# Linear attention's queries, keys and decays with features on partitions, and the last stage of an encoder block begun ahead of the last expert's rows

## The chip, the cores and the metric

The kernel runs on one core of one Trainium2 chip, in float32. The metric is the device time of one execution in microseconds (us). Before the change the median of three runs is 1846.63 us (1843.77 to 1850.55).

## What is computed

One layer of a hybrid encoder over 2048 tokens of width 1024, and a last normalisation:

```python
u = rms_norm(x, norm1_w)
z = u @ w_in + b_in            # q_a k_a (256 each), v_a g_a (512 each), lr_a (16), q_b (512), k_b v_b (128 each)
log_a = log_sigmoid(lr_a @ gla_w_a2 + gla_b_a2) / 16
# gated linear attention, 4 heads, in chunks of 64 tokens:
b = cumsum(log_a, within the chunk)
q_dec = q_a * dk**-0.5 * exp(b);  k_inv = k_a * exp(-b);  k_end = k_a * exp(b_last - b)
att   = causal(q_dec @ k_inv.T)
o     = att @ v_a + q_dec @ state;  state = exp(b_last) * state + k_end.T @ v_a
# sliding-window attention of q_b, k_b, v_b with ALiBi and sinks, 8 heads, softmax
h = x + concat(norm_gate(o, g_a), o_b) @ w_out
h = h + hier_moe(rms_norm(h, norm2_w))      # top 1 of 4 groups, top 2 of its 8 experts (SwiGLU, 512 wide)
y = rms_norm(h, final_norm_w)
```

## The kernel before

Four stages follow each other.

**Mixer.** A software pipeline over 16 tiles of 128 tokens. In iteration i each engine runs its own program (`pe_iter`, `act_iter`, `dve_iter`, `pool_iter`, `sp_iter`); the part marked new or lag 0 works on tile i, the part marked old (lag 1) on tile i-1, and lag 2 on tile i-2. The table `JOBS` lists the PSUM results in the order in which TensorE makes them; result k goes into bank k % 8, and TensorE waits until the bank's former content has been read. In one iteration TensorE does, in this order: q and k of linear attention (`qk`, tokens on partitions, 8 matmuls 512 wide, `project`, L295), transposes of the decayed q and k (`qdki`, L338 and L340), transposes of h (`u2Ta`, `u2Tb`), the chunk's scores (`att0`, `att1`, L354), the state's increments (`dS0`, `dS1`, L365), then v, router, transposed softmax rows, g, the two attentions' outputs, k_b and v_b, q_b with the low-rank gate inside it (`la`, L458), the output projection (`wo0`, `wo1`, L323), the window's scores (`s0` to `s3`, L472), and last the cumulative sums of the log decays as matmuls with constant triangles (`bb`, L482) and their chunk ends (`bl`, L486).

VectorE (DVE) ends an iteration with the second half of `h_sb` (L796), the gate (L799), the window's scores into `sc` (L807), their maxima (L814 to L819, which gives `nm_ready`), and begins the next with `qd`, `ki` and `ke` (L684 to L686), q and k times the decays. ScalarE (ACT) computes the decays `E` after the gate's exponential (L585, L586), then the eight exponentials of the softmax (L593), which wait for `nm_ready`, and begins the next iteration with the copy of the transposed `qdkiT` out of PSUM (L508), for which `att0` waits.

**Routing** makes for each of the 32 experts a list of rows: 128 in full, and up to 32 more as quarters of rows.

**Experts.** A loop over 32 experts. SyncE (SP) streams the next expert's three matrices of 2 MB while TensorE multiplies: gate (L1190), up (L1201), down (L1226, and L1215 for more than 128 rows). GpSimd (POOL) gathers rows of the normalised `v2` and adds the results into `h_dram` by two indirect DMAs per expert (`put_back`, L1109).

**Last stage** (`finish`). It begins when all 32 experts' sums have landed:

```python
sp.wait_ge(sem("h_summed"), 1)     # POOL gives it once the last expert's sums have landed
fin_sp(sp)                         # loads h_dram in 4 pieces (L1333), stores 16 tiles (L1336)
```

ACT squares and sums each tile (L1348), adds epsilon (L1351), POOL takes the power -0.5 (L1341), DVE scales by it and the weight (L1357), and SP stores. The loaded tiles lie in the weights' buffer `wts` and in `h_rest`.

## Time and profile before

| | us |
|---|---|
| median of 3 runs | 1846.63 (1843.77 to 1850.55) |
| profiled execution | 1847.37 |
| its span in the profile | 1845.5 |
| TensorE busy | 1740.8 (94%) |
| DVE, ACT, POOL busy | 579.1, 522.4, 279.9 |
| mean granted TensorE clock | 0.976 of full speed |

In the page each engine's busy time is a share of the span; one engine near its whole span in a stretch bounds the stretch, and where none is, a wait or the DMA does. The mixer is in the first half of the span, the experts in most of the second, and the last stage behind TensorE's last matmul.

### The profile page before, as it was taken

Reading aid. Unit: us, or ns where it says so; the run is one execution under the profiler, and the core shown is the slowest. Engines: PE = TensorE matmul, PEld = TensorE weight load, DVE = VectorE, ACT = ScalarE, POOL = GpSimd, SP = SyncE. Lnnn points to the kernel's source line nnn. Section 1 sums busy time; section 2 is a strip of 40 time slices with the busy share of each in tenths; the row PEclk is TensorE's granted clock in tenths of the full one; section 3 lists DMA queues with packets and bytes.
Section 4 is the critical chain, followed back from the end, with each engine's and each line's share of the span. In section 5 each row is a group of like instructions: output and inputs, shape, how many; then the busy total and the mean of one; then the engine's idle time right before and its main releaser. Section 6 shows DMA issues by size and latency. Waiting matters only on the chain. (4 is left out here: it accounts for less than half of the span.)

```text
span 1845.5 us, 29515 instructions
## 1 busy us (share of the span) xinstructions
PE 1740.8 (94%) x10686; PEld 1233.6 (67%) x10687; DVE 579.1 (31%) x1521; ACT 522.4 (28%) x1317; POOL 279.9 (15%) x345
## 2 busy tenths in 40 slices
PE   7899999999999999999976999999999999999980
PEld 4556665566656666566645788878888888888860
DVE  1344344443455334553346111111111111111114
ACT  0444343443434433434334111111111111111114
POOL 0000011010110101001010122222221222222213
PEclk9999999999999999999987999999999999999995
DMA  9410011100111001111023889989999999999969
GB/s 351 108 58 35 29 51 57 57 34 23 57 57 57 34 23 57 57 48 43 23 87 131 271 275 339 298 291 319 335 317 300 304 336 316 312 311 311 304 198 366
DMA packets 130356, 321.92 MB, mean 174 GB/s; under 512 B 10723, under 2 KB 18804, under 8 KB 130324
## 3 DMA queue, kind: packets, MB, share of 16 engines
q1 hardware_dynamic: 113908, 278.78, 42.7%
q0 software_dynamic: 15552, 42.61, 9.2%
q8 instruction: 21, 0.34, 0.1%
q10 hardware_dynamic: 864, 0.10, 0.0%
q14 instruction: 11, 0.09, 0.0%
HBM read 274.27 MB, written 47.19 MB: 174 GB/s over the span
## 5 line engine op out<-in xcount | busy, mean ns | idle before, releaser
L295 PE MATMUL bank<-w_in_sb,uT 128*128 128x512 f32 (+1 forms) x1024 | 378.9, 524 | 2.3 <-DVE uT L659 2.3
L295 PEld LDWEIGHTS bank<-w_in_sb,uT 128*128 128x128 f32 x1024 | 176.0, 191 | 169.2 <-issue 169.2
L1190 PEld LDWEIGHTS bank<-xT,wts 128*128 128x128 f32 x2048 | 248.9, 191 | 25.2 <-issue 20.8
L1190 PE MATMUL bank<-xT,wts 128*128 128x128 f32 (+2 forms) x2048 | 253.3, 283 | 6.3 <-issue 5.2
L1201 PE MATMUL bank<-xT,wts 128*128 128x128 f32 (+2 forms) x2048 | 247.9, 282 | 0.0
L1201 PEld LDWEIGHTS bank<-xT,wts 128*128 128x128 f32 x2048 | 245.0, 191 | 0.0
L1226 PE MATMUL bank<-wts,hT 128*128 128x512 f32 x512 | 231.7, 595 | 0.0
L323 PE MATMUL bank<-w_out_sb,mixT 128*128 128x512 f32 x512 | 222.7, 592 | 1.5 <-ACT mixT L536 0.8
L1279 DVE TENSOR_TENSOR hT<-bank,sg 128x160 f32<-128x160 f32 x128 | 41.6, 325 | 444.2 <-PE bank L1201 444.2
L323 PEld LDWEIGHTS bank<-w_out_sb,mixT 128*128 128x128 f32 x512 | 96.0, 190 | 116.5 <-issue 114.3
L1226 PEld LDWEIGHTS bank<-wts,hT 128*128 128x128 f32 x512 | 92.2, 190 | 97.6 <-issue 97.6
L301 PEld LDWEIGHTS bank<-uT,w_in_sb 128*128 128x128 f32 x1280 | 147.9, 192 | 11.9 <-issue 11.6
L301 PE MATMUL bank<-uT,w_in_sb 128*128 128x128 f32 x1280 | 155.7, 277 | 0.0
L830 POOL TENSOR_SCALAR ss<-ss 128x1 f32<-128x1 f32 (+1 forms) x49 | 9.4, 191 | 826.0 <-ACT junk L579 428.6
L1245 ACT ACTIVATE y<-bank,gatec 128x256 f32<-128x256 f32 x32 | 15.2, 474 | 343.8 <-PE bank L1226 197.7
L1109 POOL DMA_INDIRECT h_dram<-y,putc x64 | 102.0, 1594 | 35.9 <-POOL putc L1116 26.2
L1116 POOL COPY putc<-put 128x2 int32 (+1 forms) x32 | 5.8, 182 | 535.2 <-DVE y L1287 535.2
L1236 ACT ACT_TABLE_LOAD x32 | 41.1, 1283 | 157.9 <-PE bank L1190 157.9
L1236 ACT ACTIVATE sg<-bank 128x160 f32<-128x160 f32 x128 | 38.9, 304 | 118.3 <-PE bank L1190 117.9
L593 ACT ACTIVATE sc<-sc,sm 128x192 f32<-128x192 f32 x128 | 56.3, 441 | 33.0 <-DVE sm L819 33.0
L579 ACT ACTIVATE junk<-h_sb 128x1024 bf16<-128x1024 f32 x16 | 16.9, 1057 | 138.1 <-DVE h_sb L796 138.1
L1287 DVE TENSOR_SCALAR y<-bank,gatec 128x512 f32<-128x512 f32 x32 | 24.0, 751 | 94.3 <-PE bank L1226 94.3
(231 smaller groups left out, 1745.8 us busy)
## 6 DMA issues: line engine op xcount, KB each, us to landing
wts<-w_gate_in SPq DMA_DIRECT2D x32, 2048.0 KB, 11.0
wts<-w_up_in SPq DMA_DIRECT2D x32, 2048.0 KB, 9.5
wts<-w_down_in SPq DMA_DIRECT2D x32, 2048.0 KB
x_sb<-x_in SPq DMA_DIRECT2D x17, 512.0 KB, 3.5
xT_in<-x_t_in SPq DMA_DIRECT2D x17, 512.0 KB, 4.4
w_in_sb<-w_in_in SPq DMA_DIRECT2D x4, 2048.0 KB, 11.8
h_sb<-x_in SPq DMA_DIRECT2D x16, 512.0 KB, 3.2
h_dram<-h_sb SPq DMA_DIRECT2D x16, 512.0 KB, 2.9
```

Source lines behind the costliest of these rows:

```text
L295: m = pe.matmul(bk[name][:, col:col + hi - lo], uT[:, k, :], w_in[:, k, lo:hi], start=k == 0, stop=k == KD - 1)
L301: m = pe.matmul(bk[name][0:hi - lo, col:col + P], w_in[:, k, lo:hi], uT[:, k, :], start=k == 0, stop=k == KD - 1)
L323: m = pe.matmul(bk[f"wo{n}"][:, :], mixT[:, k, :], w_out[:, k, n * 512:(n + 1) * 512], start=k == HA, stop=k == HA - 1)
L579: act.activation(junk[:, :], h[:, 1 - par, :], ACT.Square, accum_out=ss[:, 8:9]).then_inc(sem("ss2_ready"), 1)
L593: act.activation(sc[:, hh, :], sc[:, hh, :], ACT.Exp, bias=nm[:, hh:hh + 1], accum_out=sums[:, hh:hh + 1])
L1109: po.indirect_dma_start(out=table, out_offset=bass.IndirectOffsetOnAxis(ap=putc[:, col:col + 1], axis=0), in_=src, in_offset=None, compute ...
L1190: m = pe.matmul(G[m_ % 2][:, 0:w], wg[:, k, m_ * P:(m_ + 1) * P], xT[:, k, 0:w], start=k == 0, stop=k == KD - 1)
L1201: m = pe.matmul(U[m_ % 2][:, 0:w], wu[:, k, m_ * P:(m_ + 1) * P], xT[:, k, 0:w], start=k == 0, stop=k == KD - 1)
L1226: m = pe.matmul(YB[half][:, :], hT[:, k, 0:P], wd[:, k, half * 512:(half + 1) * 512], start=k == 0, stop=k == KF - 1)
L1236: act.activation(sg[:, m_, 0:n_], G[m_ % 2][:, 0:n_], ACT.Silu).then_inc(sem(pre + "sg_ready"), 1)
L1279: nc.vector.tensor_tensor(hT[:, m_, 0:n_], U[m_ % 2][:, 0:n_], sg[:, m_, 0:n_], ALU.mult)\
L1287: nc.vector.tensor_scalar(y[:, part, 512:D], (YB, G)[part][1][:, :], gatec[:, part:part + 1], None, ALU.mult)\
```

## The change

In the mixer, q and k of linear attention come out of TensorE with features on partitions and tokens along the row (four groups of 8 matmuls 128 wide, weights stationary), and the low-rank gate `la` likewise (2 matmuls 128 wide for 1 of 256). The cumulative sum within a chunk then runs along the row: a scan on DVE over 256 elements, with a constant `within` that is 0 at each chunk's start, in place of the matmuls `bb` and `bl`, and one more DVE operation for b_last - b. ACT's exponentials of the decays move from behind the gate's last exponential to ahead of the square of h. DVE multiplies q and k by the decays at the end of the same iteration, ahead of `sc`; the first two products are written straight into `qdkiT`, so that ACT's copy of it goes. Only the third, `keT`, is still transposed (2 transposes for 4), and ACT copies it to `ke` (256 wide for 512), for which `dS0` waits. One bias table of 9 columns replaces a broadcast of 256 KB, and two constants go.

At the end, the loops of ACT, DVE and POOL stop one expert earlier and the last expert is written out. SP loads h into a buffer of its own once the sums of the first 31 experts have landed (`m_y_put` at 32 * 31), and the 16 tiles are normalised and stored from it; rows of the last expert are stored in a stale form in this pass. The last expert's up to 160 rows of h are gathered by two indirect DMAs (`pool_base`), its results are added from PSUM in SBUF (`dve_base`), normalised there, and stored over the stale rows by two indirect DMAs (`pool_out`), which wait until all 16 tiles' stores have landed. Epsilon is added on POOL, and the power is taken for up to three tiles at a time. A branch `redo` repeats the stage where experts overflow.

```diff
 JOBS = [
-    ("qk", 0, {"qk_ready": (1, 1)}), ("qdki", 1, {"qdkiT_ready": (1, 1)}),
+    ("qk", 0, {"qk_ready": (1, 1)}), ("keT", 1, {"ke_ready": (1, 1)}),
...
-    ("bb", 0, {"decays_ready": (1, 1)}), ("bl", 0, {"dec_ready": (1, 1)}),
+    ("spare0", -1, {"uT_ready": (2, 2)}), ("spare1", -1, {"uT_ready": (2, 2)}),
...
-            project("qk", C_QK, C_V).then_inc(sem("qk_done"), 1)
...
+            for n in range(4):
+                m = project_T("qk", C_QK + n * P, C_QK + (n + 1) * P, n * P)
+            m.then_inc(sem("qk_done"), 1)
+        if on("keT"):
+            wait(pe, sem("keT_ready"), i)
+            transposes("keT", lambda c: keT[:, c * P:(c + 1) * P], 2)
...
-                    pe.matmul(bk["la"][:, 0:QKA], lrT[:, :], w_a2[:, :], start=True, stop=True).then_inc(sem("la_done"), 1)
+                    for n in range(2):
+                        la = pe.matmul(bk["la"][:, n * P:(n + 1) * P], w_a2[:, n * P:(n + 1) * P], lrT[:, :], start=True, stop=True)
...
-        if on("bb"):
...
-            for n in range(2):
-                m = pe.matmul(bk["bb"][:, n * QKA:(n + 1) * QKA], cums[:, n, :], ls[:, :], start=True, stop=True)
...
-                m = pe.matmul(bk["bl"][:, 2 * pr:2 * pr + 2], ls[:, pr * P:(pr + 1) * P], cind[:, :],
...
# act_iter
-            act.activation(qdkiT[:, :, :].rearrange("p a b -> p (a b)"), BK["qdki"][:, :], ACT.Copy)\
+            wait(act, sem("keT_done"), i)
+            wait(act, sem("dS_done"), 2 * (i - 1))
+            act.activation(ke[:, :], BK["keT"][:, 0:QKA], ACT.Copy).then_inc(sem("ke_ready"), 1)
...
+            wait(act, sem("cum_ready"), 2 * i + 2)
+            wait(act, sem("keT_ready"), i)
+            act.activation(E[:, 0, :], cum[:, :], ACT.Exp, scale=1.0 / 16.0)
+            act.activation(E[:, 2, :], cum[:, :], ACT.Exp, scale=-1.0 / 16.0)
+            act.activation(E[:, 1, :], E[:, 1, :], ACT.Exp, scale=1.0 / 16.0).then_inc(sem("decays_ready"), 1)
...
# dve_iter
+            dve.tensor_tensor_scan(cum[:, :], within[:, :], ls[:, :], 0.0, ALU.mult, ALU.add).then_inc(sem("cum_ready"), 1)
...
+            wait(v_, sem("decays_ready"), i + 1)
+            wait(v_, sem("og_done"), 2 * i)
+            wait(v_, sem("keT_done"), i)
...
+            dve.tensor_tensor(keT[:, :], qk[:, QKA:], E[:, 1, :], ALU.mult).then_inc(sem("keT_ready"), 1)
...
# finish
+    PIECES = ((0, 1), (1, 4), (4, 10), (10, 16))
+    ROOTS = ((0, 1), (1, 4), (4, 7), (7, 10), (10, 13), (13, 16))
...
+    def pool_base(po):
+        po.indirect_dma_start(out=base[:, :], in_=scratch["h"], out_offset=None, in_offset=at(main)).then_inc(sem("last_moved"), 16)
+        po.indirect_dma_start(out=base_t[:, :], in_=quarters(scratch["h"]), out_offset=None, in_offset=at(rest)).then_inc(sem("last_moved"), 16)
+
+    def dve_base(v_):
+        v_.wait_ge(sem("last_moved"), 32)
+        v_.wait_ge(sem("m_d_done"), 3 * NE - 1 + CREDIT)
...
+        v_.wait_ge(sem("m_d_done"), 3 * NE + CREDIT)
+        nc.vector.scalar_tensor_tensor(base[:, H:D], bank[7][:, :], weight[:, main], base[:, H:D], ALU.mult, ALU.add).then_inc(sem("last_summed"), 1)
...
+    def pool_out(po):
+
+        po.wait_ge(sem("out_stored"), 16 * NT)
+        po.wait_ge(sem("last_steps"), 5)
+        po.indirect_dma_start(out=A["out"], out_offset=at(main), in_=last[:, :], in_offset=None, bounds_check=SEQ - 1, oob_is_err=False)\
...
# SP, then ACT behind the loop over 31 experts
-            sp.wait_ge(sem("h_summed"), 1)
-            fin_sp(sp)
...
+            sp.wait_ge(sem("m_y_put"), 32 * (NE - 1))
+            fin_sp(sp, 0)
...
+            act_silu(act, "m_", NE - 1)
+            fin_act(act, 0, 0, 4)
+            act_squares(act, 0, 2)
+            fin_act(act, 0, 4, 6)
+            act_squares(act, 2, 3)
+            fin_act(act, 0, 6, NT)
```

On DVE, at the end of an iteration of the mixer's loop, the program of before reads (`sm` holds the maxima, `qd`, `ki`, `ke` the decayed products):

```order
L796 TENSOR_TENSOR h_sb<-bank,h_sb 128x512
L799 SCALAR_TENSOR_TENSOR g_t<-g_sb,g_t 128x512
L60 REGISTER_ALU
L807 SCALAR_TENSOR_TENSOR sc<-bank,alibi 128x2x192
...
L814 TENSOR_REDUCE sm<-sc 128x8
L816 TENSOR_TENSOR sm<-sm,sinks_sb 128x8
L818 TENSOR_TENSOR sm<-sinks_sb,sm 128x8
L819 TENSOR_SCALAR sm<-sm 128x8
L684 SCALAR_TENSOR_TENSOR qd<-qk_sb,decays 128x256
L685 TENSOR_TENSOR ki<-qk_sb,decays 128x256
L686 TENSOR_TENSOR ke<-qk_sb,decays 128x256
```

and that of the change, at the same place:

```order
L780 TENSOR_TENSOR h_sb<-bank,h_sb 128x512
L783 SCALAR_TENSOR_TENSOR g_t<-g_sb,g_t 128x512
L788 SCALAR_TENSOR_TENSOR qdkiT<-qk_sb,decays 128x256
L790 TENSOR_TENSOR qdkiT<-qk_sb,decays 128x256
L792 TENSOR_TENSOR keT<-qk_sb,decays 128x256
L60 REGISTER_ALU
L800 SCALAR_TENSOR_TENSOR sc<-bank,alibi 128x2x192
...
L807 TENSOR_REDUCE sm<-sc 128x8
L809 TENSOR_TENSOR sm<-sm,sinks_sb 128x8
L811 TENSOR_TENSOR sm<-sinks_sb,sm 128x8
L812 TENSOR_SCALAR sm<-sm 128x8
```

The three products moved from behind the maxima to ahead of the window's scores.

On ACT, from the gate's logarithm to the next iteration's first copy, before:

```order
L575 ACTIVATE g_t<-g_t 128x512
L579 ACTIVATE junk,ss<-h_sb 128x1024
L582 ACT_TABLE_LOAD
L582 ACTIVATE g_t<-g_t 128x512
L585 ACTIVATE decays<-bank 128x512
L586 ACTIVATE decays<-bank 128x256
L589 ACTIVATE dec<-bank 128x4
L593 ACTIVATE sc,sm<-sc,sm 128x192 x8
L594 ACTIVATE sm<-sm 128x8
L508 ACTIVATE qdkiT<-bank 128x512
```

and of the change:

```order
L558 ACTIVATE g_t<-g_t 128x512
L562 ACT_TABLE_LOAD
L562 ACTIVATE decays<-cum 128x256
L563 ACTIVATE decays<-cum 128x256
L564 ACTIVATE decays<-decays 128x256
L566 ACTIVATE dec<-cum 128x4
L570 ACTIVATE junk,ss<-h_sb 128x1024
L573 ACTIVATE g_t<-g_t 128x512
L576 ACTIVATE sc,sm<-sc,sm 128x192 x8
L577 ACTIVATE sm<-sm 128x8
L493 ACTIVATE ke<-bank 128x256
```

The decays and the table load moved ahead of the square of h (`junk,ss<-h_sb`), and the copy behind the softmax is now that of `ke`.

On ACT, what stands behind the loop over 31 experts in the changed program (`last_sum` and `last_quarters_sum` hold the last expert's rows); before, the silu rows `sg<-bank` were in the loop and the 16 squares stood behind it:

```order
L1231 ACTIVATE sg<-bank 128x160 x4
L1362 ACTIVATE fjunk,fs<-h_back 128x1024 x4
L1388 ACTIVATE last_junk,last_means<-last_quarters_sum 128x256
L1388 ACTIVATE last_junk,last_means<-last_sum 128x512
L1362 ACTIVATE fjunk,fs<-h_back 128x1024 x2
L1388 ACTIVATE last_junk,last_means<-last_sum 128x512
L1362 ACTIVATE fjunk,fs<-h_back 128x1024 x10
```

Four squares now stand ahead of the first operation that needs the last expert's down projection, and ten behind the last one.

## Rows read from the trace of the kernel before

**Rows 1.** Windows: length, PE, PEld, DVE, ACT, POOL busy; granted clock, DMA share, GB/s.

```profile
67.00:69.00 2.00, 2.00 (x3) 0.80 (x3) 1.91 (x8) 0.00 (x0) 0.00 (x0) 0.50 1.08 381
480.00:538.00 58.00, 58.00 (x324) 35.90 (x323) 25.64 (x71) 22.57 (x59) 5.23 (x8) 1.00 0.12 45
1783.00:1795.00 12.00, 8.97 (x36) 4.75 (x34) 2.86 (x6) 1.05 (x2) 1.26 (x2) 1.00 0.01 3
1804.00:1845.50 41.50, 0.00 (x0) 0.00 (x0) 20.02 (x16) 21.67 (x48) 14.44 (x16) 0.50 0.99 397
```

**Rows 2.** Timeline of TensorE in the mixer's steady loop (start, duration, what, records).

```profile
519.40 1.57 PE L472 MATMUL bank<-kb_sb,qbT 64*128 64x192 f32 x16
520.90 1.13 PE L482 MATMUL bank<-la_t,cums 128*128 128x256 f32 x4
522.23 7.11 PE L295 MATMUL bank<-w_in_sb,uT 128*128 128x512 f32 x16
529.18 0.38 PE L338 MATMUL bank<-ident,qd 128*128 128x128 f32 x2
...
530.59 0.46 PE L354 MATMUL bank<-qdkiT 64*64 64x64 f32 x16
530.87 0.65 PE L365 MATMUL bank<-v_sb,ke 64*64 64x128 f32 x16
531.45 7.13 PE L295 MATMUL bank<-w_in_sb,uT 128*128 128x512 f32 x16
...
557.35 3.74 PE L301 MATMUL bank<-uT,w_in_sb 128*128 128x128 f32 x32
561.01 0.69 PE L458 MATMUL bank<-w_a_sb,lrT 17*128 17x256 f32 x2
561.64 2.05 PE L301 MATMUL bank<-uT,w_in_sb 128*128 128x128 f32 x16
```

**Rows 3.** Timeline of ACT in the same iteration.

```profile
520.23 1.06 ACT L579 ACTIVATE junk<-h_sb 128x1024 bf16<-128x1024 f32 x1 [8.67 <-DVE h_sb L796]
...
523.71 0.38 ACT L586 ACTIVATE decays<-bank 128x256 f32<-128x256 f32 x1
...
526.16 0.45 ACT L593 ACTIVATE sc<-sc,sm 128x192 f32<-128x192 f32 x1 [2.01 <-DVE sm L819]
...
529.82 0.60 ACT L508 ACTIVATE qdkiT<-bank 128x512 f32<-128x512 f32 x1
```

**Rows 4.** Timeline of DVE, then of POOL, in the same iteration.

```profile
524.88 1.25 DVE L819 TENSOR_SCALAR sm<-sm 128x8 f32<-128x8 f32 x1
526.04 0.41 DVE L684 SCALAR_TENSOR_TENSOR qd<-qk_sb,decays 128x256 f32<-128x256 f32 x1
...
526.71 0.41 DVE L686 TENSOR_TENSOR ke<-qk_sb,decays 128x256 f32<-128x256 f32 x1
...
524.82 1.28 POOL L854 TENSOR_TENSOR gm<-gm,gnorm_sb 128x512 f32<-128x512 f32 x1
```

**Rows 5.** Timeline of TensorE in iteration 1, with the wait ahead of it.

```profile
65.08 0.46 PE L354 MATMUL bank<-qdkiT 64*64 64x64 f32 x16 [2.94 <-ACT qdkiT L508]
...
66.00 8.83 PE L295 MATMUL bank<-w_in_sb,uT 128*128 128x512 f32 x16
```

**Rows 6.** DMA issues of 1770 to 1776 us: expert 30's sums (median us to landing).

```profile
h_dram<-y,putc POOLq DMA_INDIRECT x2, 8.5
```

**Rows 7.** Timelines of POOL and SP at the end, then the chain's DMA, then SP's last wait.

```profile
1773.34 1.57 POOL L1109 DMA_INDIRECT h_dram<-y,putc  x1 [0.30 <-issue]
...
1793.92 1.60 POOL L1109 DMA_INDIRECT h_dram<-y,putc  x1 [0.82 <-POOL putc L1116]
...
1801.85 1.36 SPq L1333 DMA_DIRECT2D wts<-h_dram  x3
...
1800.81 0.50 POOLq L1406
...
SPq L1364 <- DMA out<-h_rest: 5.3, 1, 5.3
```

More of the change, by code:

```diff
@@ L1353, in dve_tiles @@
-    def dve_tiles(v_):
-        v_.wait_ge(sem("fw_loaded"), 16)
-        for t in range(NT):
-            v_.wait_ge(sem("froot_ready"), t + 1)
-            nc.vector.scalar_tensor_tensor(hc[t], hc[t], fs[:, t, 1:2], K["fw"][:, :], ALU.mult, ALU.mult)\
-                .then_inc(sem("sum_o_ready"), 1)
-    return sp_first, dve_first, sp_tiles, pool_tiles, act_tiles, dve_tiles
+            sp.wait_ge(sem("sum_o_ready"), NT * turn + t + 1)
+            sp.dma_start(A["out"][t * P:(t + 1) * P, :], hc[:, t, :]).then_inc(sem("out_stored"), 16)
@@ new lines, in root, with pool_roots @@
+    def root(po, mean, dst, nth, ready):
+        nc.gpsimd.tensor_scalar(mean, mean, 1.0, EPS, ALU.mult, ALU.add).then_inc(sem("mean_steps"), 1)
+        po.wait_ge(sem("mean_steps"), 3 * NT + 1 + nth)
+        nc.gpsimd.tensor_tensor(dst, mean, K["power"][:, 0:mean.shape[-1]], ALU.pow).then_inc(sem(ready), 1)
+    def pool_roots(po, turn, first, end):
+        for n, (lo, hi) in list(enumerate(ROOTS))[first:end]:
+            po.wait_ge(sem("fss_ready"), NT * turn + hi)
+            root(po, fs[:, 0, lo:hi], fs[:, 1, lo:hi], len(ROOTS) * turn + n + 1 + (turn or n >= 3), "froot_ready")
@@ new lines, in act_tiles, with dve_tiles @@
+    def act_tiles(act, turn, lo, hi):
+        for t in range(lo, hi):
+            for n, (first, _) in enumerate(PIECES):
+                if first == t:
+                    act.wait_ge(sem(f"h_back{n}"), 16 * (turn + 1))
+            if NT * turn + t >= 2:
+                act.wait_ge(sem("fss_ready"), NT * turn + t - 1)
+            act.activation(fjunk[:, t % 2, :], hc[:, t, :], ACT.Square, scale=D ** -0.5, accum_out=fs[:, 0, t:t + 1])\
+                .then_inc(sem("fss_ready"), 1)
+    def dve_tiles(v_, turn, lo, hi):
+        v_.wait_ge(sem("fw_loaded"), 6 * 16)
+        for t in range(lo, hi):
+            v_.wait_ge(sem("froot_ready"), len(ROOTS) * turn + 1 + [t < end for _, end in ROOTS].index(True))
+            nc.vector.scalar_tensor_tensor(hc[:, t, :], hc[:, t, :], fs[:, 1, t:t + 1], K["fw"][:, :], ALU.mult, ALU.mult)\
+                .then_inc(sem("sum_o_ready"), 1)
@@ new lines, in act_squares, with pe_quarters @@
+    def act_squares(act, lo, hi):
+        parts = (base_t[:, :], ljunk[:, 0:Q]), (base[:, 0:H], ljunk[:, Q:Q + H]), (base[:, H:D], ljunk[:, Q + H:Q + D])
+        for n in range(lo, hi):
+            act.wait_ge(sem("last_summed"), n + 1)
+            act.activation(parts[n][1], parts[n][0], ACT.Square, scale=D ** -0.5, accum_out=fp[:, n:n + 1]).then_inc(sem("last_squares"), 1)
+    def pe_quarters(pe):
+        pe.wait_ge(sem("fw_loaded"), 6 * 16)
+        pe.wait_ge(sem("last_squares"), 2)
+        pe.matmul(bank[0][:, 0:2], quad[:, :], fp[:, 0:2], start=True, stop=True).then_inc(sem("last_squares"), 1)
@@ L1500, in _ @@
                 dve_y(v_, "m_", e, 0)
+            dve_h(v_, "m_", NE - 1)
+            dve_x(v_, NE, range(3))
+            fin_dve(v_, 0, 0, 4)
+            dve_base(v_)
+            fin_dve(v_, 0, 4, 7)
+            dve_means(v_)
+            fin_dve(v_, 0, 7, 10)
+            dve_scale(v_)
+            fin_dve(v_, 0, 10, NT)
             def over(j):
```

242 lines of the change are left out of this document (133 added, 109 removed).

## The prediction

> **What bounds the kernel now.** I read the busy shares by windows first, then TensorE's timeline of one steady iteration of the mixer, then ACT's and DVE's of the same stretch, and last everything behind TensorE's last matmul.
>
> In the mixer TensorE is busy 58.00 of 58 us at full granted clock while DVE and ACT are busy 25.64 and 22.57 [rows 1]. What TensorE issues there is what an iteration costs, as long as each operand is ready when its turn comes. Its operands come from two serial chains, and the one that matters starts when the output projection ends (I call that moment W, 519.40, when the window's scores start [rows 2]): DVE adds h, gates, makes `sc`, takes maxima; ACT then does eight exponentials from 526.16 and is free at 529.82, when it copies `qdkiT` [rows 3]; TensorE starts `att` at 530.59 [rows 2]. So ACT is free at W + 10.42, a moment that the change doesn't move by itself.
>
> In the experts' loop nothing is changed. The end is bound otherwise: between 1783 and 1795 the DMA engines stand idle (share 0.01) while the last expert is computed, and from 1804 to 1845.5 they are busy 0.99 at 397 GB/s, with DVE and ACT busy half of it [rows 1]. The last stage is 8.4 MB in and 8.4 MB out, and DMA sets its length: from SP's first load at 1801.85 to the last store's landing, some 43.4 us (SP waits 5.3 us for it at the very end, up to about 1845.2) [rows 7].
>
> **TensorE's terms, per iteration.** Start to start in [rows 2]:
> - `bb` and `bl` go: 520.90 to 522.23, -1.33.
> - `qk`: 8 matmuls 512 wide take 522.23 to 529.18, 6.95. The new form is that of L301, of which 16 take 557.35 to 561.01, 3.66; 32 take 7.32. +0.37.
> - The 12 transposes from 529.18 to 530.59 take 1.41, 0.118 each; two go: -0.24.
> - `la`: 1 matmul 256 wide takes 561.01 to 561.64, 0.63; two of 128, at L301's 0.229 each, 0.46. -0.17.
>
> Together -1.37 if TensorE never waits. The trained eye asks here whether narrow matmuls are as cheap per column as wide ones: 7.32 against 6.95 says nearly. The Trainium skill (TensorE: Matmul & The Clock Gate, Back-to-back issue gap) gives sustained spacings of about 81 ns for 128 columns and 131 ns for 512, so four narrow ones would cost 2.5 times a wide one; scaled to these 6.95 that would be some 17 us instead of 7.3. It has a rival below, and this trace speaks against it.
>
> **The wait that the change makes.** `att` now needs only DVE's products, ready long before. `dS` needs `ke`, which ACT copies behind the softmax. TensorE comes to `dS` at W + 1.50 (scores) + 7.32 + 0.24 (`keT`) + 0.94 (8 transposes) + 0.28 (`att`, 530.59 to 530.87) = W + 10.28. `ke` is ready at W + 10.42 + 0.38 (a 256 wide copy from PSUM, as L586 [rows 3]) + 0.1 to 0.2 until TensorE starts (the copy of `qdkiT` ended at 530.42, `att` started at 530.59) = W + 10.95. So a new wait of 0.67; `v` starts at W + 11.53 (`dS` takes 0.58, 530.87 to 531.45) where it started at W + 12.05. Gain 0.52, with `la` 0.69 per iteration.
>
> That stands on ACT being free when it was. Two things move on the way there. DVE's three products, 0.335 each (526.04 to 526.71 for two, [rows 4]), now stand ahead of `sc`: +1.01. Against it, L819 of 8 columns took 1.25 us, from 524.88 to the end of POOL's L854 (524.82 + 1.28) [rows 4]: it stood still behind POOL. With the table load and the decays out of the way, ACT gives the gate's exponential about 1.3 us earlier (from 521.29 to 523.71 [rows 3] it now does that load and two exponentials of 0.5 to 0.6 each), POOL's two products end by about 524.8, and L819, starting at 525.9, should take about 0.2. The maxima are then ready at 526.1, as now. I take a shift of 0; its bounds are -0.2 and +1.1 (the stall stays). The rule behind it is in the Trainium skill (SBUF — State Buffer, SBUF: two separate sides): a DVE operation in a two-port mode and a GpSimd operation exclude each other for a whole instruction; the row agrees.
>
> Hidden: the scan and the subtraction on DVE stand ahead of `uT`, which TensorE needs only at W + 1.5, and DVE idles there later. No row shows a scan of 256; the nearest, 256 wide products of 0.41 [rows 4], bound it from below, and even at 2 us it ends some 10 us before W. I take 0. The decays on ACT: it stands idle for 8.67 us until h comes at 520.23; a table load, the gate's exponential and all the decays now take 2.8 together (521.29 to 524.09) [rows 3]. So they end some 5 us ahead of W, and the count of table loads stays. Cost 0; if they came after W they would delay `sc` one for one. Fewer bytes at the start (a 256 KB broadcast): between 0 and 1 us, I take 0.
>
> Iterations: 15 of 16. Iteration 0 has no old tile and waits for weights, and in the drain behind tile 15 the chain, not TensorE, sets the pace. 15 x 0.69 = **-10.4**.
>
> **The end, step by step.** SP now waits for expert 30's sums. The second DMA of the pair is issued at 1773.34 [rows 7] and lands a median 8.5 us later [rows 6]: 1781.9, plus 0.3 until SP issues. The stage's 43.4 us then run in the idle stretch: 1782.2 + 43.4 = 1825.6. The gathers of the last expert's rows add 0.65 MB, 1.6 us at 397 GB/s: 1827.2. Does compute keep up? TensorE ends near 1792 (8.97 us busy from 1783), and an ACT tile costs at most 1.35 us (21.67 / 16), a DVE tile 1.25 (20.02 / 16) [rows 1]. ACT stops ahead of tile 4 until DVE has scaled tiles 1 to 3 (loaded near 1791, scaled near 1799) and added the last expert's rows, and is at tile 6 near 1804. Ten tiles end by 1817.5, the power and three scalings by 1823, a few us ahead of 1827. DMA stays the bound, by little.
>
> Then new work on the path: the two indirect stores. Now such a pair takes from 1793.92 to its landing, 1800.81 [rows 7], 6.9 us, with accumulation; a plain write may save up to 2. I take 6.9: 1834.1, against 1845.2. **-11.1**; bounds -8 (a longer tail, ACT behind the DMA) and -14.
>
> **Sum.** 1847.37 - 10.4 - 11.1 = 1825.9. The profiled execution lies 0.7 above the median of the runs shown, so **1825** for the median.
>
> **The rivals.** A measurement of this kernel can tell about 0.5%, 9 us, from no change.
> - *TensorE doesn't wait for `ke`* (the chain is 0.7 us shorter, as L816 and L819 both stop waiting for POOL): 15 x 1.37 = 20.6, with 11.1 at the end: 1815. For it: L819 may cost less than 0.2; against it: the eight exponentials and the maxima keep their length. 0.15.
> - *The stall of L819 stays, or the chain is otherwise 0.7 us later:* the mixer gains nothing, 1836; 1.1 later gives 1842. 0.14.
> - *The end gains little:* stores wait behind loads and ACT is late because it stands still twice; -4 instead of -11: 1832. 0.10.
> - *The change doesn't do what it says at the end* (expert 30's sums land late, or the loads delay expert 31, so that the stage isn't ahead): only the mixer's gain less the 6.9 of the indirect stores, 1843. 0.03.
> - *The chain to `ke` becomes the mixer's bound, and slower than before.* Each us that `ke` is later costs 15 us. The kernel is slower by more than 9 us from a delay of (9 + 10.4 + 11.1) / 15 = 2.0 us per iteration. There TensorE would wait 2.7 us, and at a wait of 2.94 in iteration 1 [rows 5] the granted clock stood at 0.50, the 1.2 GHz level, from 67 to 69 [rows 1]: `v` took 8.83 for 6.95. With that, 15 x (2.0 + 1.9) on top of the forecast: 1884. For it: two DVE operations more ahead of the maxima's end and in-order ACT; against it: 5 us of slack where the decays are made. 0.03.
> - *Narrow matmuls cost what the skill's spacing says:* in rows, `qk` would have to take 17 where L301 shows 7.3: 16 x 10 = +160, less 20, some 1985. 0.01, since L301 is the same form in the same loop.
> - The forecast: 0.54.
>
> **How the numbers follow.** The forecast's own range is 1818 to 1832. To hold 8 in 10 it must take in the first rival (1815, with its own spread down to 1812) and most of the second: 1812 to 1836. Faster by over 0.5% (below 1837): the forecast, the first and third rival, and two thirds of the second, 0.88; within 0.5%: 0.08; slower: 0.04.
>
> **What would show it.** In the profile after: iterations 0.7 us shorter; `qk` 7.3 us; a wait of 0.5 to 0.9 ahead of `dS`, released by ACT's copy of `ke`, and none ahead of `att`; L819's successor short (0.2 us); DVE's products at W + 1.3. At the end: SP's first load some 10 us before TensorE's last matmul, DMA above 0.9 throughout, the last plain store landed about 35 us behind TensorE's end, and some 7 us of indirect stores behind it. The forecast is wrong if `dS` waits over 1.5 us, if DMA shows gaps between loads and stores, or if TensorE loses clock in the steady iterations.

## The result, and the profile after

The changed kernel took 1828.63 us (median of 4 runs, 1828.08 to 1829.92) beside 1845.82 us for the kernel before (4 runs, 1843.77 to 1850.55). The ratio is 0.9905, 95% interval 0.9891 to 0.9920: faster by 17.2 us where 21.5 were forecast. The profiled execution took 1828.53 us, its span 1826.5 us, 19.0 less than before's.

Stage by stage, from the start of one named group of TensorE's to the start of the next, in the two profiled executions (us):

| stretch | before | after | change |
|---|---|---|---|
| start to iteration 1's output projection | 98.02 | 102.83 | +4.8 |
| from there to iteration 15's (14 iterations) | 815.03 | 804.00 | -11.0 |
| drain, up to the routing's first matmul | 61.90 | 60.86 | -1.0 |
| routing, up to the first expert's rows | 33.83 | 33.61 | -0.2 |
| experts, up to the last 8 matmuls | 779.59 | 778.30 | -1.3 |
| from there to the end of the span | 57.13 | 46.90 | -10.2 |

So the steady iterations and the end gave about what was forecast, and the start of the mixer lost what nobody had on the bill.

**A steady iteration.** The changed kernel's window, as the second of [rows 1]:

```profile
480.00:538.00 58.00, 57.70 (x376) 39.32 (x371) 25.94 (x74) 22.47 (x60) 5.33 (x8) 1.00 0.13 46
```

TensorE's timeline, same place in the program as [rows 2]:

```profile
518.66 1.57 PE L470 MATMUL bank<-kb_sb,qbT 64*128 64x192 f32 x16
520.16 7.41 PE L299 MATMUL bank<-uT,w_in_sb 128*128 128x128 f32 x64
527.41 0.38 PE L288 MATMUL bank<-ident,keT 128*128 128x128 f32 x2
527.63 1.04 PE L288 MATMUL bank<-ident,h_sb 128*128 128x128 f32 x8
528.60 0.46 PE L350 MATMUL bank<-qdkiT 64*64 64x64 f32 x16
529.36 0.67 PE L361 MATMUL bank<-v_sb,ke 64*64 64x128 f32 x16 [0.30 <-ACT ke L493]
```

W is 518.66 here. `bb` and `bl` are gone: `qk` starts 1.50 behind W, not 2.83. It takes 7.25 us, start to start. Then the forecast wait: `dS` starts at W + 10.70, held by ACT's `ke`. Of the 58 us 0.30 are idle. The period went from 58.22 to 57.43 (the second row of the table, by 14).

ACT's, then DVE's timeline of that iteration:

```profile
525.23 0.45 ACT L576 ACTIVATE sc<-sc,sm 128x192 f32<-128x192 f32 x1 [4.07 <-DVE sm L812]
...
528.85 0.36 ACT L493 ACTIVATE ke<-bank 128x256 f32<-128x256 f32 x1
...
520.65 0.42 DVE L792 TENSOR_TENSOR keT<-qk_sb,decays 128x256 f32<-128x256 f32 x1
520.98 1.94 DVE L800 SCALAR_TENSOR_TENSOR sc<-bank,alibi 128x384 f32<-128x384 f32 x4
...
525.03 0.17 DVE L812 TENSOR_SCALAR sm<-sm 128x8 f32<-128x8 f32 x1
```

The three products stand ahead of `sc`, and L812, which was L819 with its 1.25 us in [rows 4], takes 0.17. The first exponential starts at W + 6.57; it was W + 6.76 [rows 3].

**Iteration 1.** The place of [rows 5] in TensorE's timeline:

```profile
62.34 0.46 PE L350 MATMUL bank<-qdkiT 64*64 64x64 f32 x16
68.83 1.13 PE L361 MATMUL bank<-v_sb,ke 64*64 64x128 f32 x16 [6.03 <-ACT ke L493]
69.89 9.72 PE L293 MATMUL bank<-w_in_sb,uT 128*128 128x512 f32 x16
```

And its windows, the granted clock being the third number from the end:

```profile
66.00:70.00 4.00, 1.17 (x17) 0.87 (x17) 1.48 (x4) 2.69 (x14) 0.00 (x0) 0.50 0.70 246
70.00:74.00 4.00, 4.00 (x5) 1.74 (x6) 3.76 (x11) 0.00 (x0) 0.00 (x0) 0.50 0.02 4
```

The wait is 6.03 where it was 2.94, the granted clock then stands at 0.50 (1.2 GHz) from 66 to 74 us, and `v` takes 9.72 (8.83 before, 7.1 in a steady iteration). DVE's rows of iteration 0 say why the wait is so long there:

```profile
56.41 0.69 DVE L783 SCALAR_TENSOR_TENSOR g_t<-g_sb,g_t 128x512 f32<-128x512 f32 x1 [1.75 <-ACT g_t L558]
58.75 0.42 DVE L788 SCALAR_TENSOR_TENSOR qdkiT<-qk_sb,decays 128x256 f32<-128x256 f32 x1 [1.65 <-ACT decays L564]
```

In iteration 0 there is no output projection. The decays, which ACT makes long before W in a steady iteration, are here the last thing to come: DVE stands 1.65 us for them, then spends 1.0 on the products, and only then begins `sc`. All of this is ahead of the maxima and so of `ke`.

**The end.** The timelines, as in [rows 7], of SP, TensorE, ACT, DVE and POOL, and in the last line the last plain store in the chain that ended last:

```profile
1772.74 2.29 SPq L1340 DMA_DIRECT2D h_back<-h_dram  x4
1779.60 3.60 PE L1221 MATMUL bank<-wts,hT 128*128 128x512 f32 x8
1791.67 0.42 ACT L1388 ACTIVATE last_junk<-last_quarters_sum 128x256 bf16<-128x256 f32 x1 [5.36 <-DVE last_quarters_sum L1379]
1798.10 3.68 DVE L1369 SCALAR_TENSOR_TENSOR h_back<-h_back,fs,fw 128x1024 f32<-128x1024 f32 x3 [5.14 <-POOL fs L1348]
1820.73 1.06 POOL L1414 DMA_INDIRECT out<-last_rows,put  x1 [12.05 <-DMA out<-h_back]
1816.77 3.12 DMA out<-h_back
```

Its windows (granted clock, DMA share and GB/s last):

```profile
1795.00:1805.00 10.00, 0.00 (x0) 0.00 (x0) 4.52 (x6) 10.00 (x22) 3.63 (x8) 0.50 1.03 415
1805.00:1818.00 13.00, 0.00 (x0) 0.00 (x0) 11.74 (x11) 1.13 (x4) 3.51 (x3) 0.50 0.87 346
```

SP's loads start 6.9 us ahead of the last group of matmuls and 10.5 ahead of its end (1783.2). Up to 1805 the DMA share is full. Behind it is 0.87, while DVE is busy 11.74 of 13 us: DVE has become the one that is waited for. From TensorE's end it is 36.7 us to the last plain store's landing (1819.9), and 6.6 more to the end of the span; POOL issues the first indirect store 0.8 after that landing.

### The profile page after: what moved, and what is told of

It is laid out like the page before. It is cut to its first block, busy times and chain, and to the rows that moved or that the text cites. A ratio compares the mean times of both kernels' runs of the same rounds, so it can differ in the third digit from the quotient of the medians.

```text
span 1826.5 us, 30836 instructions
## 1 busy us (share of the span) xinstructions
PE 1723.8 (94%) x11328; PEld 1282.4 (70%) x11329; DVE 581.0 (32%) x1558; ACT 515.0 (28%) x1319; POOL 276.6 (15%) x344
## 4 chain that ended last, share of the span: by engine, by line
PE 83%; DVE 7%; ACT 5%; issue 2%; DMA 2%; POOL 0%; DVEq 0%; ACTq 0%; POOLq 0%; SPq 0%
PE bank L293 14%; PE bank L1185 13%; PE bank L1196 13%; PE bank L321 12%; PE bank L1221 12%; PE bank L299 9%; ACT sc L576 3%; PE bank L1153 2%; PE bank L288 2%; DVE sc L800 2%; DVE sm L807 2%; PE bank L1210 1%; PE bank L959 1%; PE bank L376 1%; PE bank L419 1%
## 5 line engine op out<-in xcount | busy, mean ns | idle before, releaser
L299 PE MATMUL bank<-uT,w_in_sb 128*128 128x128 f32 x2304 | 277.0, 279 | 3.3 <-DVE uT L642 3.3
L299 PEld LDWEIGHTS bank<-uT,w_in_sb 128*128 128x128 f32 x2304 | 266.3, 194 | 15.5 <-issue 13.3
L293 PE MATMUL bank<-w_in_sb,uT 128*128 128x512 f32 (+1 forms) x768 | 264.1, 497 | 0.0
L293 PEld LDWEIGHTS bank<-w_in_sb,uT 128*128 128x128 f32 x768 | 128.0, 191 | 112.0 <-issue 112.0
L1257 DVE TENSOR_TENSOR xT<-bank,norm_sb 128x128 f32<-128x128 f32 x66 | 16.1, 286 | 115.5 <-PE bank L1153 115.5
## 6 DMA issues: line engine op xcount, KB each, us to landing
wts<-w_gate_in SPq DMA_DIRECT2D x32, 2048.0 KB, 11.1
```

Of the source, the lines that this page charges most:

```text
L293: m = pe.matmul(bk[name][:, col:col + hi - lo], uT[:, k, :], w_in[:, k, lo:hi], start=k == 0, stop=k == KD - 1)
L299: m = pe.matmul(bk[name][0:hi - lo, col:col + P], w_in[:, k, lo:hi], uT[:, k, :], start=k == 0, stop=k == KD - 1)
```

## The experiments

**The two halves alone.** The mixer of the changed kernel with the finish of before, and the other way round. The second keeps GpSimd's semaphores of the changed mixer, with the same instructions.

```diff
-def finish(nc, sem, bank, A, K, scratch, ctx):
+def finish(nc, sem, A, K, scratch, W, ctx):
...
```

This is the first against the changed kernel, with the body and the calls of before; in the second the functions `mixer` and `loads` are those of before.

> The mixer's part of the change with the finish of before. Theory A (the two parts add; the mixer's part is 14 iterations of -0.75 us, +4.8 us lost in iterations 0 and 1, and 0 to -2.4 us between the drain and the last expert): the router's last matmuls of the drain start near 934.6 us, TensorE's last expert matmul ends 6.4 to 8.8 us earlier than before's 1792, and the time is 1837 to 1839.5 us. Rival (the end hides it, because the last stage is bound by its own DMA and starts from something that the mixer does not move): over 1843 us. Rival (the mixer's part is smaller without the other, because the 2.4 us behind the drain come from the finish): 1839.4 us, with TensorE's end 6.4 us earlier only.

> The finish's part of the change with the mixer of before (GpSimd's semaphores of the changed kernel, same instructions). Theory A (the parts add): TensorE's end stands at before's 1792 us, or up to 2.4 us ahead of it if the gain behind the drain comes from this part; from that end to the end of the span 43.3 us in place of before's 53.5; the time is 1833 to 1836 us. Rival (the early start of the final loads slows the last expert's weights or scatters): TensorE's last expert is over 0.5 us longer than before's and the time is over 1838 us. The two parts' gains added should give the whole's 17.2 us within 2 us.

The mixer alone took 1839.48 us, ratio 0.9961 (0.9948 to 0.9974); the finish alone 1838.37 us, ratio 0.9951 (0.9930 to 0.9973). In us of 1845.6 that is -7.2 and -9.0, together -16.2 beside the whole's -17.5 (0.0095 of it): they add, within intervals of 2.4 and 4 us to either side. In the traces the split is sharper. From the start of the last 8 matmuls to the end of the span it takes 46.6 us in the second kernel (1792.04 to 1838.6) and 57.4 in the first (1780.26 to 1837.7); 46.9 and 57.1 in the kernels after and before. So the end's gain belongs to the finish alone, and needs nothing from the mixer. TensorE's last group stood 8.1 us ahead of before's in the first kernel, 6.4 to 8.8 were expected. Its time lies at the upper end of the expected 1837 to 1839.5, where the second rival's 1839.4 lies too; that rival had 6.4 us for the group, and the 8.1 speak against it.

The finish alone missed its 1833 to 1836, by its median; its six runs spread from 1832.24 to 1841.17. In the profiled one, 1840.60, that group stood 3.7 us behind before's. 1.8 of these are there ahead of iteration 1's output projection, and another 1.8 in the experts (781.42 in place of 779.59), though neither part was edited. The next paragraph takes that up. The rival, that the early loads slow the last expert, names a time over 1838, which was met, and an expert over 0.5 us longer, which was not: from the last matmuls of the expert before it to its own it takes 22.3 us (1769.79 to 1792.04), and 22.5 in the kernel before (1765.88 to 1788.37).

**What varies without an edit.** Some stretches differ from one execution to the next where nothing was changed. The first scores of iteration 0 start at 51.0 and 52.1 us in the two kernels with the mixer of before; in the changed kernel at 52.2, and in the seven others with narrow `qk` at 50.8 to 52.0. So the +1.2 us that the two traces show up to there is no more than what varies, and no price of narrow matmuls. From these scores to iteration 1's output projection the numbers do separate: 47.0 and 47.8 in the kernels with the old mixer, 49.9 to 50.6 in the six with the new one whose chain to `ke` is unaltered. By the means the loss at the start is 2.9 us, not 4.8. Part of the 2.9 is the clock: the granted clock is below 1.00 in one window of 4 us (66 to 70, 0.57) in the kernel before, and in all four from 62 to 78 in the changed one.

The experts take 777.6 to 779.6 us in eight of the ten kernels with the same q and k, and 781.4 and 781.9 in e2_finish_alone and e6_no_last_stores; in these two, and in none of the eight, a stretch of over 3 us (from 1064.8 and from 1054.5) stands at a granted clock of 0.50. The routing takes 33.6 to 33.8 us in five of all eleven kernels and 35.1 to 36.1 in the other six; why is open. The end, from TensorE's last group on, takes 46.6 to 47.0 in the four kernels with the changed kernel's finish and its q and k, so that a difference of 1 us can be told there. The drain takes 61.8 and 61.9 with the old mixer and 60.5 to 60.9 with the new one as it is, so its 1 us is the mixer's.

**`ke` copied by another engine.**

```diff
-# act_iter, behind the exponentials of the iteration before
-            act.activation(ke[:, :], BK["keT"][:, 0:QKA], ACT.Copy).then_inc(sem("ke_ready"), 1)
...
+# dve_iter, ahead of the wait for exps_ready
+            wait(v_, sem("keT_done"), i)
+            wait(v_, sem("dS_done"), 2 * (i - 1))
+            dve.tensor_copy(ke[:, :], BK["keT"][:, 0:QKA]).then_inc(sem("ke_ready"), 1)
```

> The changed kernel with the copy of `ke` from PSUM on VectorE, ahead of its wait for the exponentials, in place of ScalarE behind them. Theory A (TensorE's wait at `dS` hangs on the chain maxima, 8 exponentials, copy): the wait of 0.30 us in a steady iteration goes, so does the period's 0.30 us (57.42 to 57.12; 14 times, -4.2 us); in iteration 1 `dS` starts near 65.2 us in place of 68.83 and the clock does not fall for so long, -4.5 to -6 us; in the drain the 5.7 us wait goes but nothing ends earlier, because the router's matmuls wait for VectorE's work behind the exponentials: 0. Sum -9 to -10 us: 1818 to 1820 us. Rival B (the wait at `dS` only shows a slack that the next wait takes over, at `v` or at the first transposes of the probabilities): the wait moves there, the period stays within 0.1 us of 57.42, and the time is over 1824 us.

1816.16 us, ratio 0.9838 (0.9815 to 0.9861): 12.5 us less than the changed kernel. TensorE's timeline at the same place of the iteration:

```profile
516.84 0.46 PE L350 MATMUL bank<-qdkiT 64*64 64x64 f32 x16
517.12 0.62 PE L361 MATMUL bank<-v_sb,ke 64*64 64x128 f32 x16
```

And the window of one period:

```profile
470.00:526.90 56.90, 56.90 (x366) 38.81 (x365) 25.99 (x74) 22.28 (x60) 5.33 (x8) 1.00 0.12 46
```

No wait is left: TensorE is busy the whole period, 56.91 us. That is 0.52 less than 57.43, where the row of the wait says 0.30. The rest is in the rows too: with the wait, 0.76 us pass from the start of `att` to that of `dS` (528.60 to 529.36), without it 0.28. The rows show where: without the wait, `dS` starts 0.18 us ahead of the end of `att` (517.12, and 516.84 + 0.46 = 517.30), and with it 0.30 behind that end (529.36, and 529.06). So a wait costs the time shown and the overlap that is lost, 0.48 together. In iteration 1 the wait fell to 2.36 us, now for DVE, the granted clock stayed at 1.00 (62 to 82 us) and `v` took 7.13:

```profile
63.75 0.67 PE L361 MATMUL bank<-v_sb,ke 64*64 64x128 f32 x16 [2.36 <-DVE ke L661]
64.35 7.13 PE L293 MATMUL bank<-w_in_sb,uT 128*128 128x512 f32 x16
```

From iteration 0's scores to iteration 1's output projection it is now 43.9 us. Theory A holds, rival B falls. The sum was too small by 3 us, 14 times 0.2 of it for the lost overlap. The drain gave nothing, as expected: from iteration 15's output projection to the routing 60.3 us (60.9), with TensorE then waiting 5.69 at the router's matmuls.

**The products behind the maxima.**

```diff
-            wait(v_, sem("decays_ready"), i + 1)
...
-            dve.tensor_tensor(keT[:, :], qk[:, QKA:], E[:, 1, :], ALU.mult).then_inc(sem("keT_ready"), 1)
             wait(v_, sem("pTc1_done"), i)
...
             dve.tensor_scalar(nm, m_, -1.0, None, ALU.mult).then_inc(sem("nm_ready"), 1)
+            wait(v_, sem("decays_ready"), i + 1)
...
+            dve.tensor_tensor(keT[:, :], qk[:, QKA:], E[:, 1, :], ALU.mult).then_inc(sem("keT_ready"), 1)
```

> The changed kernel with VectorE's three products (q, k and ke with their decays) behind the maxima and not ahead of the scores' sums. Theory A (the products lengthen the chain to `ke` by 1.0 us in a steady iteration and, with the wait for the decays, by 2.7 us in iteration 0): the negated maxima are ready 0.6 to 0.7 us earlier in a steady iteration (the small operation that makes them falls inside GpSimd's second product and may wait 0.35 us for its end), the wait of 0.30 us at `dS` goes (-4.2 us in 14 iterations), iteration 1 gains 2.7 to 3.5 us, the drain 0 to 1.0 us: 1820 to 1822 us. Rival B (the last small operation stalls until GpSimd's second product is over, as in the kernel before with 1.25 us, and takes all that the earlier start gives): it takes over 1.0 us again, the maxima are no earlier, the wait at `dS` stays 0.2 to 0.4 us, and the time is 1824 to 1826 us.

1816.70 us, ratio 0.9840 (0.9817 to 0.9862). The period is 56.91 here as well: the same bound, reached from the other side. Timelines of DVE and POOL; W is 511.80:

```profile
516.88 0.48 DVE L799 TENSOR_TENSOR sm<-sm,sinks_sb 128x8 f32<-128x8 f32 x1
...
517.48 0.17 DVE L802 TENSOR_SCALAR sm<-sm 128x8 f32<-128x8 f32 x1
...
516.07 1.27 POOL L849 TENSOR_TENSOR gm<-gm,gnorm_sb 128x512 f32<-128x512 f32 x1
```

The maxima end at W + 5.85, 0.69 earlier than in the changed kernel (W + 6.54). An operation on 8 columns takes 0.17, but the one that starts while POOL's second product runs takes 0.48 and ends with it (517.36 and 517.34). The same is seen in [rows 4], longer. That is the lock of the Trainium skill (SBUF — State Buffer, SBUF: two separate sides): of a GpSimd operation that reads SBUF and a DVE one with two SBUF inputs (or in a two-port mode, which L819 with its one input would have to be in), whichever starts first keeps the port for its whole length. The trace agrees, with 0.31 us here and 1.08 in the kernel before. Rival B falls: the stall was 0.31, not 1.25, since the operation came late in POOL's product and not at its start. In iteration 0 the edit takes the decays' wait and the products out of the way of the maxima, and from the scores to iteration 1's output projection it takes 47.7 us, as with the old mixer (47.0 and 47.8) and not 49.9 to 50.6: what the start lost, it lost there. The time was 3 us better than the best that was expected, and the 14 periods gave 7.2 in place of 4.2: the lost overlap again.

**Wide `qk`.** TensorE's timeline and then, in a fence of its own, its window stand behind the edit.

```diff
-            for n in range(4):
-                m = project_T("qk", C_QK + n * P, C_QK + (n + 1) * P, n * P)
-            m.then_inc(sem("qk_done"), 1)
+            project("qk", C_QK, C_V).then_inc(sem("qk_done"), 1)
```

> The changed kernel with q and k projected as before, 8 pairs of 512 columns in place of 32 pairs of 128; what is read as q, k with features on partitions is then other numbers (and the linear attention's rows of the output with them), the instructions behind are the same. The projection should take 6.95 us in place of 7.25 in a steady iteration. Theory A (a steady iteration is set by the chain from the output projection's end over the maxima and the exponentials to `ke`, so that TensorE's work ahead of `dS` is covered): the wait at `dS` grows from 0.30 to about 0.60 us, the period stays at 57.42 us within 0.05, and the time is 1828 to 1829 us. Rival B (the shown wait is no part of the period's bound): the period falls by 0.30 us, 15 times, 1824 us.

```profile
519.19 7.13 PE L293 MATMUL bank<-w_in_sb,uT 128*128 128x512 f32 x16
526.16 0.38 PE L288 MATMUL bank<-ident,keT 128*128 128x128 f32 x2
...
528.38 0.67 PE L359 MATMUL bank<-v_sb,ke 64*64 64x128 f32 x16 [0.57 <-ACT ke L491]
```

```profile
480.00:538.00 58.00, 57.43 (x323) 35.35 (x322) 25.54 (x73) 23.09 (x63) 5.32 (x8) 1.00 0.13 50
```

`qk` takes 6.97 (519.19 to 526.16) and the wait grew to 0.57, by just what was saved: TensorE is idle 0.57 in 58 us, no longer 0.30. From iteration 1's output projection to the router's matmuls of the drain it takes 831.8 us (101.83 to 933.63), in the changed kernel 831.75 (102.83 to 934.58). So the chain sets the iteration, and narrow `qk` costs it nothing: A holds, for the mixer. The time, 1835.53 us, is no measure of it. The experts took 789.8 us in place of 778.3, and the end 43.2 in place of 46.9. What they do hangs on how many rows each expert gets, which the other q and k may well have changed through the router; no run here shows it.

**The order of the last stage.**

```diff
-            act_squares(act, 0, 2)
-            fin_act(act, 0, 4, 6)
-            act_squares(act, 2, 3)
-            fin_act(act, 0, 6, NT)
+            act_squares(act, 0, 3)
+            fin_act(act, 0, 4, NT)
...
-            fin_dve(v_, 0, 0, 4)
+            fin_dve(v_, 0, 0, 1)
             dve_base(v_)
-            fin_dve(v_, 0, 4, 7)
+            fin_dve(v_, 0, 1, 4)
             dve_means(v_)
-            fin_dve(v_, 0, 7, 10)
+            fin_dve(v_, 0, 4, NT)
             dve_scale(v_)
-            fin_dve(v_, 0, 10, NT)
```

> The changed kernel with another order in the last stage alone: VectorE adds the last expert's rows to the gathered ones in its idle time behind tile 0, and scales them behind tile 15; ScalarE squares them behind tile 3, ahead of tile 4. Theory A (from 1805 us on the last stage waits for VectorE, which is late because both engines stand idle for 5 us while tiles 4 to 9 lie loaded): ScalarE starts tile 4 near 1791 us on the changed kernel's time scale in place of 1792.96, VectorE's scaling of tile 15 starts near 1809 us in place of 1815.5, the DMA share stays near 1.0 until the last plain store is issued, and from TensorE's last expert matmul to the end of the span it takes 40 to 41 us in place of 43.3; the time is 1825.5 to 1826.5 us. Rival B (the last stage is bound by its DMA bytes alone, and the low shares behind 1805 us are only the tail of the queues): the same 43.3 us within 0.5, 1828 to 1829 us.

Measured 1828.50 us, ratio 0.9903 (0.9880 to 0.9927), not told from the changed kernel's. In the trace, TensorE's last group to the end of the span takes 45.8 us (1780.00 to 1825.8) in place of 46.9. Timelines of ACT, DVE and POOL, then the windows:

```profile
1791.20 1.06 ACT L1362 ACTIVATE fjunk<-h_back 128x1024 bf16<-128x1024 f32 x1 [2.99 <-DMA h_back<-h_dram]
1804.86 7.26 DVE L1369 SCALAR_TENSOR_TENSOR h_back<-h_back,fs,fw 128x1024 f32<-128x1024 f32 x6 [1.02 <-POOL fs L1348]
1819.98 1.06 POOL L1414 DMA_INDIRECT out<-last_rows,put  x1 [11.93 <-DMA out<-h_back]
```

```profile
1805.00:1818.00 13.00, 0.00 (x0) 0.00 (x0) 8.72 (x8) 0.64 (x2) 2.24 (x2) 0.50 0.98 400
1818.00:1820.00 2.00, 0.00 (x0) 0.00 (x0) 0.00 (x0) 0.00 (x0) 0.02 (x1) 0.50 0.03 12
```

The steps of theory A are there: tile 4 at 1791.2, the DMA share 0.98 up to 1818, DVE done with its tiles 4.6 us earlier (1812.1 and 1816.7; the last one began at 1810.85, where some 1809 was expected). But the end gained 1.1 us, not 2.3 to 3.3: with DVE done at 1812.1, the last store still landed at 1819.1, behind a stretch in which the DMA was full, and not quite at its end (share 0.03 behind 1818). DVE as the bound cost 1.1 us, and e9_all, with the same order, has it again (45.7). Both theories had half of it.

**Without the two indirect stores.** They and SyncE's wait for them are left out:

```diff
         po.wait_ge(sem("out_stored"), 16 * NT)
         po.wait_ge(sem("last_steps"), 5)
-        po.indirect_dma_start(out=A["out"], out_offset=at(main), in_=last[:, :], in_offset=None, bounds_check=SEQ - 1, oob_is_err=False)\
...
+        po.nop()
...
-            sp.wait_ge(sem("last_moved"), 64)
+            sp.wait_ge(sem("last_moved"), 32)
```

> The changed kernel without its two last indirect stores, so that the rows of the last expert stay in the output without its sum; SyncE's last wait counts two indirect transfers fewer. It prices the serial end. Theory A (the two stores stand alone behind the last plain store): the span ends where GpSimd's wait for the plain stores ends, 5.8 us less: TensorE's end to the span's end 37.5 us in place of 43.3. Rival (part of the 5.8 us is the end of the program, and stays): 2 to 4 us less.

One run with its profile. From the last group's start to the end of the span it takes 44.4 us (1782.98 to 1827.4) in place of 46.9: 2.5 us less, not 5.8. SP meets the last plain store's landing at 1822.9 (39.9 behind the last group's start; 40.3 in the changed kernel), and the span ends at 1827.4. What stands between is shown by the view of the program's closing line in this kernel (engine, instruction, count, ns least/median/most, start):

```profile
L1428 SPq COMPARE_BRANCH  x1: 38/38/38, 1822.9 to 1822.9; - x1
L1428 POOLq DRAIN  x1: 3057/3057/3057, 1824.1 to 1824.1; - x1
L1428 SPq EVENT_SEMAPHORE  x1: 17/17/17, 1827.3 to 1827.3; - x1
```

All engines meet at the end of the program, and POOL drains for 3.06 us before it does. The drain begins at 1824.1, when its own wait for the plain stores is over and 1.2 us of its control instructions have run. The same view of the changed kernel:

```profile
L1431 POOLq DRAIN  x1: 4032/4032/4032, 1822.3 to 1822.3; - x1
L1431 SPq COMPARE_BRANCH  x1: 38/38/38, 1824.5 to 1824.5; - x1
```

There the indirect stores had landed at 1824.4, and POOL's drain ran until 1826.3. That asked for one more kernel, in which POOL doesn't wait either:

```diff
-        po.wait_ge(sem("out_stored"), 16 * NT)
         po.wait_ge(sem("last_steps"), 5)
         po.nop()
```

> e6_no_last_stores (the two last indirect stores left out, so that the last expert's rows of the output lack its sum), and in addition GpSimd no longer waits for the plain stores; SyncE still does. In e6 the profile shows GpSimd's own drain at the end of the program, 3.06 us from 1824.1, begun when its wait for the plain stores was over, and the span ends with it. Theory A (that drain, and not a DMA, is what ends the span whenever GpSimd waits for the stores): it now lies beside the stores, and from the start of TensorE's last 8 matmuls to the end of the span it takes 40.2 us, in place of 44.4 in e6 and 46.9 in the changed kernel; the indirect stores with GpSimd's part in them are then worth 6.7 us. Rival (some end of the program of 3 to 4 us stands behind the last store on whatever engine waits for it, here SyncE): 43.5 to 44.5 us.

```profile
L1427 POOLq DRAIN  x1: 3053/3053/3053, 1812.6 to 1812.6; - x1
L1427 SPq COMPARE_BRANCH  x1: 38/38/38, 1821.4 to 1821.4; - x1
L1427 SPq EVENT_SEMAPHORE  x1: 17/17/17, 1821.7 to 1821.7; - x1
```

40.7 us (1781.08 to 1821.8): the drain of 3.05 us lies beside the stores and the span ends 0.4 behind SP's wait. 40.2 were expected, and the rival's 43.5 to 44.5 falls. So the pair of stores costs 6.2 us (46.9 less 40.7), of which 2.5 go with the stores and 3.7 with POOL's late end. Counted from the last plain store's landing (1819.9, 1822.85 and 1821.4) to the end of the span, which leaves out what varies ahead of it, the three kernels have 6.6, 4.5 and 0.4 us: 2.1 and 4.1. Each of the three is one execution. The rival of e6_no_last_stores had its 2 to 4 us right and a cause too broad: what stays is POOL's drain, not an end on whichever engine.

**All together.** As in e3, and in addition, in ScalarE's and in VectorE's iteration:

```diff
+            if isinstance(i, int) and i == 0:
+                act.wait_ge(sem("keT_done"), 1)
+                act.activation(ke[:, :], BK["keT"][:, 0:QKA], ACT.Copy).then_inc(sem("ke_ready"), 1)
             wait(act, sem("nm_ready"), i + 1)
...
+            if isinstance(i, int) and i == NT:
+                u2T_block()
             wait(v_, sem("exps_ready"), i)
```

`u2T_block` holds the two operations that write u2T; VectorE copies `ke` from iteration 2 on, and the last stage has the order of e5.

> All that helps together: `ke` copied by VectorE as in e3_ke_on_dve, that of iteration 1 by ScalarE ahead of iteration 0's exponentials, VectorE's two operations that write u2T in the first iteration of the drain ahead of its wait for the exponentials, and the last stage in the order of e5_finish_order. Theory A (each wait read from the traces is on the path): against e3_ke_on_dve's 1816.2 us, iteration 1 gives 1.75 us (its `dS` starts near 62.0 us by that run's start, not 63.75), the drain's wait of 5.69 us at the router's matmuls goes and gives 1.3 to 3 us, the last stage 2 to 3 us: 1808.5 to 1811.5 us. The steady period stays at 56.91 us, TensorE's busy time. Rival B (behind the wait for u2T the same VectorE work is waited for at the masked scores, and the last stage is DMA bytes alone): 1814 to 1815 us.

1810.33 us (5 runs, 1809.44 to 1811.19), ratio 0.9800 (0.9780 to 0.9820): 35 us less than before and 18 less than the changed kernel, inside the expected range, though not by the steps that were expected. TensorE in iteration 1 and in the drain:

```profile
62.17 0.67 PE L361 MATMUL bank<-v_sb,ke 64*64 64x128 f32 x16 [0.17 <-ACT ke L572]
...
911.76 0.67 PE L361 MATMUL bank<-v_sb,ke 64*64 64x128 f32 x16 [2.13 <-DVE ke L672]
912.96 1.77 PE L376 MATMUL bank<-u2T,w_r_sb 128*36 128x128 f32 x16 [0.53 <-DVE u2T L665]
917.38 1.09 PE L288 MATMUL bank<-ident,g_t 128*128 128x128 f32 x4 [2.65 <-DVE sc L682]
```

From the scores to iteration 1's output projection it takes 42.6 us (43.9 in e3). In the drain the wait of 5.69 is 0.53, but 2.65 of it come back at the probabilities' transposes, and the drain takes 59.65 us (60.30 in e3): 0.65 gained, where 1.3 to 3 were expected. Moved work showed the next wait. The end gained 1.25 (46.98 in e3, 45.73), where 2 to 3 were expected. Together that is 3.1 us against e3, and the spans of the two profiled executions differ by 2.9, where 5 to 8 were expected. The medians differ by 5.8 because e3's profiled execution, 1814.14, lay 2.0 below its median; that the median fell into the range is in part luck.

## Why the prediction was right, step by step

- **TensorE's terms.** `bb` and `bl`, -1.33: exact (2.83 to 1.50 behind W). `qk`: 7.25 for 7.32. The rival of narrow matmuls fell: 7.25 narrow in the changed kernel, 6.97 wide in e8, in the same place. The `la` term was wrong: two matmuls of 128 take what one of 256 took. Rows of the changed kernel, in iteration 1:

```profile
100.08 0.71 PE L455 MATMUL bank<-lrT,w_a_sb 17*128 17x128 f32 x4
100.72 2.05 PE L299 MATMUL bank<-uT,w_in_sb 128*128 128x128 f32 x16
```

  That is 0.64, in [rows 2] 0.63; the forecast had 0.46, from matmuls with 128 rows in place of these 17. Its 0.17 per iteration were never there.
- **The new wait at `dS`.** The place, the releaser and the mechanism were right, and e3 and e4 show them from two sides. The forecast's 0.67 runs from the moment at which TensorE comes to `dS` to its start, and by that count it measured 0.48 (W + 10.22 to W + 10.70); the 0.30 in the row is counted from the end of `att`. `dS` started at W + 10.70, not 10.95, since the chain came out 0.19 shorter (first exponential at W + 6.57) and ACT was free at W + 10.19, not 10.42. DVE's shift was taken as 0 with bounds of -0.2 and +1.1, and came out at its lower bound. The products' +1.0 and the vanished stalls of L819 (1.08) and L816 (0.11) did cancel.
- **Per iteration** 0.69 was forecast, 0.79 measured, over 14 iterations -11.0 against -10.4 for 15. Two errors, 0.24 too little for the chain and 0.17 too much for `la`, nearly cancelled, which is luck.
- **Iterations 0 and 1** were the step that failed. The text let the decays be "hidden", with 5 us of slack, from a steady iteration's rows; it even named the cover (ScalarE's idle time ahead of h) and not that iteration 0 has no h to wait for. There the decays and the products are on the path, in front of a wait that already was 2.94. It cost 2.9 us by all the kernels together, and e4, which takes both out of that path, has the old length again; this pair of traces shows 4.8.
- **Drain and behind.** 0 was forecast, 1.0 gained in the drain, 1.5 behind it. The latter is inside what the experts vary (777.6 to 781.9 us over the kernels with the same q and k). It is luck that these 2.5 made up for half of what the start lost; without them the gain would have been some 15 us, still inside the range.
- **The end.** SP's loads 10.5 us ahead of TensorE's end, as forecast. The last plain store landed 36.7 us behind it, forecast 35.2. Behind that came 6.6 for the forecast 6.9, but of another kind: the indirect stores had landed after 4.5, and the other 2.1 are POOL's drain, which the forecast didn't have. "DMA stays the bound, by little" was wrong from 1805 on, and worth 1.1 us (e5). -10.2 against -11.1.
- **The rival "no wait"** (1815) is what e3 and e4 are. Each gets to 1816 with a few lines, so the forecast's 0.15 for it was a statement on where one copy stands.

## What to carry to other kernels

Price a moved operation in the first and last iterations by their own rows: what a steady iteration covers is bare where its cover is missing, and a wait there may also bring the clock down. Where TensorE waits for the last small operation of a long serial chain, look for an engine that is idle at that moment before shortening anything; one copy moved from ScalarE to VectorE was worth 12 us here, over two thirds of what the whole change gave. And when a serial tail looks expensive, leave it out in two steps, the work and then the wait ahead of it: here the engine's own end was over half of it.
